# Convolution moved into the attention stage, half of the output weights loaded there, and the first tile taken first in the expert stage

## The chip, the cores and the metric

The kernel runs on one core of a Trainium2 chip. The metric is the device time of one execution in microseconds (us). TensorE is PE in the profile (its weight loads PEld), VectorE is DVE, ScalarE is ACT, GpSimd is POOL and SyncE is SP.

## The reference, cut to what matters

A trunk of two layers works on 640 tokens of width 1024: 128 context tokens (tile 0) and 512 latent tokens (tiles 1 to 4). Each layer computes, in float32:

```
h   = rms_norm(x) * (1 + scale1) + shift1
z   = h @ w_in                                  # 1024 x 2720
o_a = rwkv7(z); o_b = latent attention(z); o_c = grouped attention(z)
u   = c_gate * x_in                             # short convolution over the tokens
o_d = b_gate * (u[t-1] * w0 + u[t] * w1 + u[t+1] * w2 + conv_b)
x   = x + gate1 * (concat(o_a, o_b, o_c, o_d) @ w_out)
h2  = rms_norm(x) * (1 + scale2) + shift2
q   = h2 @ peer_wq                              # 8 heads, two halves each
    # scores against 2 x 128 keys, the best 16 of each half, the best 16 pairs: 128 experts a token
x   = x + gate2 * sum_k gelu(U[idx_k] . h2) * share_k * V[idx_k]
```

U and V are tables of 16384 rows of 4 KB for each layer. Every token needs 128 rows of each.

## The kernel before, in words

Per layer the program runs stages one after another, each closed by a barrier of all engines (`stage`, L139): the recurrent stage, `stage_mix`, `stage_attention`, `stage_experts`. Within a stage each engine has a list of instructions written out by hand, and semaphores order the engines.

**`stage_mix` (L988).** Six steps: five token tiles and the cached context. GpSimd computes the powers of -1/2 (L1182, L1186, L1202) that normalise rows and, between them, the convolution of the tile before (`convolve`, L1164 to 1178): per tile seven operations on 128x256, three multiplications by a tap (L1174) and four that add or multiply (L1178). All read and write SBUF. They need the shifted copies of u that SP makes by DMA at the start of the stage. VectorE does the row work of each step (L1277 to 1341).

**`stage_attention` (L1368).** 40 units, a tile and a head each: scores on TensorE (L1411, L1413), the maximum (L1477) and its negative (L1479) on VectorE, the exponential on ScalarE (L1457), transposes (L1438) and the product with the values (L1423) on TensorE, the copy (L1499), the reciprocal (L1502) and the scaling (L1487) on VectorE. GpSimd has nothing to do. SP loads the gates (L1398). The eight units of the context tile have one block of 128 keys, the other 32 have five.

**`stage_experts` (L1615).** At its start:

- SP loads both halves of w_out (L1684, 2 MB each), the first block of peer_wq, the keys, the second block of peer_wq (L1685 to 1687).
- TensorE transposes o chunk by chunk, eight chunks, each for all five tiles (L1988 for tile 0, L1990 for tiles 1 to 4). ScalarE copies tile 0's part to hT (L1827), VectorE the rest (L2071).
- TensorE then makes output products 0, 1 and 2 (`output(i)`, L1935 to 1942; product i is tile i//2, half i%2; 8 matmuls of 128x512 each). VectorE multiplies each by its gate (`gate_output`, L2066) and GpSimd adds it to x (`add_output`, L1725).
- With products 0 and 1 tile 0 is done: square sum (L1783), rstd (L1729, L1732), scaling (L2075), transposes (L1956), shift and scale (L2078). VectorE's scaling stands behind the gate of product 2 in its list.
- `first(n)` makes tile 0's queries and scores for two heads (L1971, L1980). VectorE ranks them in 20 steps (`rank_step`, L1530) and gives 32 expert numbers a token.
- GpSimd then issues a gather for each expert slot (L1770): 128 rows of 4 KB, one for each token. 128 gathers of U and then 128 of V for each of the five tiles, into a ring of 13 buffers. A gather waits until the row set that it replaces is used.
- VectorE forms the dot products with U (L2087). Rows of V are summed half by TensorE (L2051), half by VectorE (L2112). Before V can be used, ScalarE takes the exponentials of tile 0's best scores (L1847). They stand in its list behind the last copy of the other tiles' scores.
- The other tiles' output products, their normalisation and their queries (L1917) and scores (L1928) are made by TensorE under tile 0's gathers. `ADD_BEFORE`, `RSTD_BEFORE` and `GATE_BEHIND` say before which gather, or behind which dot product, an add, an rstd or a gate stands.

```
ADD_BEFORE = {2: 3, 7: 4, 12: 5, 18: 6, 22: 7, 26: 8, 30: 9}
RSTD_BEFORE = {4: 1, 14: 2, 24: 3, 31: 4}
GATE_BEHIND = {1: 4, 6: 5, 12: 6, 16: 7, 18: 8, 20: 9}
```

SBUF is full, so areas are used again: `m.w[0]` and `m.w[1]` are the two halves of one area of 32 KB a partition. In the attention stage it holds queries, keys and values up to column 7168. `m.rows` holds the constants of a layer, the taps and the bias of the convolution among them. In the expert stage its first 4096 columns hold the keys, two buffers, and scores.

Of the kernel before, what the change touches and what calls it, by code (L numbers as in the profile page):

```python
# [19 lines left out]
P = 128  # L20
# [967 lines left out]
def stage_mix(nc, m, l):  # L988
# [3 lines left out]
    with stage(nc) as sem:  # L992
# [22 lines left out]
        with nc.Block() as block:  # L1015
# [145 lines left out]
            def _(eng):  # L1161
                conv = Order(eng, conv_ordered)

                def convolve(t, first, end):  # L1164

                    if t < 0:
                        return
                    before, after, u = m.conv_before[:, t, :], m.conv_after[:, t, :], m.conv_u[:, t, :]
                    if t == 0 and first == 0:
                        eng.wait_ge(shifted, 96)  # L1170
                    for k in range(first, end):
                        if k < 3:
                            ap = (after, before, u)[k]
                            conv.mark(eng.tensor_tensor(ap, ap, row(m, "conv_w", (2, 0, 1)[k] * GW, GW), ALU.mult))  # L1174
                        else:
                            other = (before, u, row(m, "conv_b"), m.z[:, t, ZB:ZB + GW])[k - 3]
                            conv.after(0)
                            conv.mark(eng.tensor_tensor(after, after, other, ALU.mult if k == 6 else ALU.add))  # L1178

# [19 lines left out]
                for i in range(STEPS):  # L1199
# [10 lines left out]
                conv.after(0)  # L1210
# [157 lines left out]
def stage_attention(nc, m, l):  # L1368
# [17 lines left out]
    with stage(nc) as sem:  # L1386
# [4 lines left out]
        gates_loaded = sem("gates_loaded")  # L1391
        inverse, done = Marks(sem("sum_inverse"), "unit"), Marks(sem("attention_done"), "unit")
        with nc.Block() as block:
            @block.sync
            def _(eng):
                for g in range(2):
                    for s in range(2):
                        eng.dma_start(m.gate[:, g, s, :], m.gates[l, g, s].partition_broadcast(P)).then_inc(gates_loaded, 16)  # L1398
                eng.wait_ge(gates_loaded, 64)

# [214 lines left out]
def stage_experts(nc, m, l):  # L1615
# [10 lines left out]
    ADD_BEFORE = {2: 3, 7: 4, 12: 5, 18: 6, 22: 7, 26: 8, 30: 9}  # L1626
    RSTD_BEFORE = {4: 1, 14: 2, 24: 3, 31: 4}
    with stage(nc) as sem:
        sems = RankSemaphores(sem)
        w_out_loaded = [sem(f"w_out_loaded{b}") for b in range(2)]  # L1630
        o_turned = Marks(sem("o_turned"), "chunk")
        o_kept_v, o_kept_a = Marks(sem("o_kept_vector"), "chunk"), Marks(sem("o_kept_scalar"), "chunk")
# [45 lines left out]
        with nc.Block() as block:  # L1678
            @block.sync
            def _(eng):  # L1680
                w_out = at_layer(m.inp["w_out"], l).rearrange("(c p) n -> p c n", p=P)
                src = at_layer(m.inp["peer_wq"], l).rearrange("(c p) n -> p c n", p=P)
                for n in range(2):
# [216 lines left out]
            def _(eng):  # L1900
# [34 lines left out]
                def output(i):  # L1935
                    t, n = i // 2, i % 2
                    if t == 0:
                        eng.wait_ge(w_out_loaded[n], 16)
# [429 lines left out]
```

## Time and profile before

| | us |
|---|---|
| median of 3 runs | 4997.46 (4996.35 to 4998.36) |
| the profiled execution | 4998.08 |
| its span | 4996.3 |

| engine | busy us | share of the span |
|---|---|---|
| TensorE | 3135.7 | 63% |
| VectorE | 3904.6 | 78% |
| ScalarE | 770.0 | 15% |
| GpSimd | 2769.8 | 55% |

The span is the time from the first to the last instruction of the profiled execution; 1.8 us lie around it. The shares are means over stages with different limits, so what a change in one stage is worth is read from that stage. The mean granted clock of TensorE is 0.843 of full speed. Layer 0's mix stage runs from 622.3 us, its attention stage from 713.6 us, its expert stage from 822.7 us.

### The profile page before, as it was taken

To read this page: it belongs to the slowest core of one execution; us is meant where nothing else is said; L and a number is where in the kernel's file an instruction comes from. 1 tells how busy PE (TensorE), PEld (TensorE's weight loads), DVE (VectorE), ACT (ScalarE), POOL (GpSimd) and SP (SyncE) were. 2 spreads that over 40 slices of the span, in tenths; PEclk is the share of its full clock that TensorE was granted. 3 is DMA by queue.
4 is the path that set the end of the run, shared out by engine and by line. 5 is a ranking of instruction groups with operands and counts; after the bars stand their busy time and mean duration, and the time that the engine had idled before them with its cause. 6 is when DMAs were issued, how large, how long until landed. Compare 5 with 4: busy or idle time off the path is not lost. (4 is left out here: it accounts for less than half of the span.)

```text
span 4996.3 us, 39271 instructions
## 1 busy us (share of the span) xinstructions
PE 3135.7 (63%) x11894; PEld 1704.7 (34%) x11894; DVE 3904.6 (78%) x7390; ACT 770.0 (15%) x1904; POOL 2769.8 (55%) x2867
## 2 busy tenths in 40 slices
PE   8989869897045063277977995989713605407237
PEld 3368836542011021023425883754201202102012
DVE  6947674998997997978754666579889799799875
ACT  2112252211010010012111224321100101001001
POOL 0013240667777777766661224056777777767776
PEclk9989969999578597598998996999966958759669
DMA  8600012899999999999993001269999999999999
GB/s 308 226 17 2 3 33 76 315 411 409 410 399 409 409 399 407 398 410 390 417 381 115 2 1 36 76 248 410 409 409 400 409 409 395 410 409 399 410 399 365
DMA packets 434889, 1491.66 MB, mean 299 GB/s; under 512 B 47212, under 2 KB 55524, under 8 KB 433910
## 3 DMA queue, kind: packets, MB, share of 16 engines
q0 software_dynamic: 368640, 1342.34, 67.7%
q1 hardware_dynamic: 66040, 146.81, 8.2%
q8 instruction: 97, 1.59, 0.1%
q14 instruction: 112, 0.92, 0.1%
HBM read 1480.92 MB, written 5.44 MB: 297 GB/s over the span
## 5 line engine op out<-in xcount | busy, mean ns | idle before, releaser
L2051 PE MATMUL ps<-z,o 128*128 128x512 f32 x2356 | 1156.4, 618 | 516.9 <-DMA z<-in_peer_v,experts 333.6
L2087 DVE CUSTOM_DVE_ANT_0 z<-z,ps 128x1024 f32<-128x1024 f32 x1176 | 1414.4, 1218 | 77.2 <-DMA z<-in_peer_u,experts 38.5
L1770 POOL DMA_INDIRECT z<-in_peer_u,experts x1176 | 1113.5, 947 | 495.4 <-issue 214.5
L1770 POOL DMA_INDIRECT z<-in_peer_v,experts x1178 | 1115.1, 947 | 443.3 <-issue 274.1
L2112 DVE SCALAR_TENSOR_TENSOR ps<-z,state,ps 128x1024 f32<-128x1024 f32 x579 | 743.0, 1283 | 330.7 <-DMA z<-in_peer_v,experts 330.4
L2051 PEld LDWEIGHTS ps<-z,o 128*128 128x128 f32 x2356 | 411.3, 192 | 1256.4 <-ACT o L1890 712.9
L1905 PE MATMUL ps<-const,hT 128*128 128x128 f32 x80 | 17.8, 396 | 1035.4 <-ACT o L1890 1035.4
L1890 ACT ACTIVATE o<-const,state 128x128 f32<-128x128 f32 x640 | 244.5, 399 | 1070.0 <-PE ps L2051 1065.4
L1905 PEld LDWEIGHTS ps<-const,hT 128*128 128x128 f32 x80 | 14.4, 207 | 1040.7 <-ACT o L1890 1019.1
L1917 PE MATMUL ps<-hT,w 128*128 128x512 f32 x512 | 223.7, 592 | 0.0
L844 POOL TENSOR_TENSOR kn<-kn,neg_half 128x4 f32<-128x4 f32 x20 | 20.1, 1007 | 341.7 <-DVE kn L887 313.1
L854 POOL TENSOR_TENSOR w<-w,const 128x512 f32<-128x512 f32 x60 | 86.6, 1449 | 220.2 <-DVE w L876 122.7
L463 DVE SCALAR_TENSOR_TENSOR o<-gate,cond,o 128x1024 f32<-128x1024 f32 x160 | 192.4, 1275 | 10.2 <-DMA gate<-in_w_mod 10.2
L854 POOL TENSOR_TENSOR hT<-hT,const 128x512 f32<-128x512 f32 x60 | 85.6, 1432 | 205.4 <-DVE hT L876 103.6
L400 PE MATMUL ps<-w,hT 128*128 128x512 f32 (+1 forms) x480 | 189.4, 552 | 4.1 <-ACT hT L322 4.1
L1884 ACT ACTIVATE state<-state 128x128 f32<-128x128 f32 x10 | 3.1, 308 | 1172.3 <-DVE state L2093 1172.3
L1725 POOL TENSOR_TENSOR x<-x,rows 128x512 f32<-128x512 f32 x20 | 26.4, 1321 | 275.8 <-DVE rows L2066 275.5
L2033 PE MATMUL ps<-w,hT 128*128 128x512 f32 (+1 forms) x384 | 148.9, 551 | 3.0 <-ACT hT L1870 3.0
L1942 PE MATMUL ps<-w,hT 128*128 128x512 f32 x320 | 143.2, 608 | 5.0 <-DMA w<-in_w_out 5.0
L1917 PEld LDWEIGHTS ps<-hT,w 128*128 128x128 f32 x512 | 95.4, 190 | 111.0 <-issue 111.0
L400 PEld LDWEIGHTS ps<-w,hT 128*128 128x128 f32 x480 | 86.5, 192 | 102.5 <-issue 98.0
L1477 DVE TENSOR_REDUCE small<-ps 128x1 f32<-128x640 f32 (+1 forms) x80 | 57.4, 718 | 70.2 <-PE ps L1413 57.0
(434 smaller groups left out, 5234.5 us busy)
## 6 DMA issues: line engine op xcount, KB each, us to landing
gate<-in_w_mod SPq DMA_DIRECT2D x80, 512.0 KB, 4.5
w<-in_w_in SPq DMA_DIRECT2D x15, 2048.0 KB, 11.4
z<-in_peer_v,experts POOLq DMA_INDIRECT x1178, 12.0
z<-in_peer_u,experts POOLq DMA_INDIRECT x1176, 13.6
w<-in_peer_wq SPq DMA_DIRECT2D x8, 2048.0 KB, 19.4
w<-in_w_out SPq DMA_DIRECT2D x4, 2048.0 KB, 10.7
z<-in_peer_wq SPq DMA_DIRECT2D x4, 2048.0 KB, 16.9
rows<-in_rows SPq DMA_DIRECT2D x2, 2272.5 KB, 14.6
```

What stands on the lines that cost most here:

```text
L400: mm = eng.matmul(m.ps[:, 4 + i % 4, 0:cols], m.hT[:, c, t * P:(t + 1) * P], m.w[n % 2][:, c, 0:cols], start=(c == 0), stop=(c == KC - 1))
L463: eng.scalar_tensor_tensor(total, m.mod_piece[i % BUFFERS], m.cond[:, c, s:s + 1], m.mod_bias if c == 0 else total, ALU.mult, ALU.add).the ...
L854: eng.tensor_tensor(heads4(m.ct[d][j % 2][:, :]), m.lh[d][:, :].rearrange("p (h k x) -> p h k x", h=4, k=2)[:, :, 0, :], bc(const(m, f"lev ...
L1477: eng.tensor_reduce(m.small[:, u % 2:u % 2 + 1], scores, AX.X, ALU.max).then_inc(most.sem, most.one("raw", u))
L1770: eng.indirect_dma_start(slot, None, at_layer_rows(table), bass.IndirectOffsetOnAxis(ap=m.experts[:, t % 2, k:k + 1], axis=0)).then_inc(lo ...
L1890: eng.activation(m.diag[:, (done + q) % DIAGS, :], const(m, "ident"), ACT.Copy, scale=m.weight[:, 2 * q:2 * q + 1]).then_inc(diags_ready, 1)
L1917: mm = eng.matmul(m.ps[:, 6 + j % 2, :], m.w[p % 2][:, c, j % PER * P:(j % PER + 1) * P], m.hT[:, c, P:TOK], start=(c == 0), stop=(c == KC ...
L1942: mm = eng.matmul(m.ps[:, 4 + i % 2, :], m.hT[:, c, t * P:(t + 1) * P], m.w[n][:, c, :], start=(c == 0), stop=(c == KC - 1))
L2033: mm = eng.matmul(m.ps[:, 6 + i % 2, 0:cols], m.hT[:, c, t * P:(t + 1) * P], m.w[n % 2][:, c, 0:cols], start=(c == 0), stop=(c == KC - 1))
L2051: mm = eng.matmul(m.ps[:, 4 + n, :], m.diag[:, (done + q) % DIAGS, :], row_j[:, n * 512:(n + 1) * 512], start=(q == 0), stop=(q == SLOTS / ...
L2087: eng.tensor_tensor_reduce(row_j, row_j, h_rows, 1.0, 0.0, ALU.mult, ALU.add, m.acts[:, k:k + 1]).then_inc(used_v, 1)
L2112: ins = eng.scalar_tensor_tensor(acc, row_j, m.weight[:, k:k + 1], acc, ALU.mult, ALU.add)
```

## The change

1. `convolve` leaves `stage_mix`. The same 35 operations a layer become GpSimd's list in `stage_attention`.
2. SP, in `stage_attention`, waits for these 35 operations and then loads the first half of w_out into the first 4096 columns of `m.rows`, which nothing reads from then on. `stage_experts` loads the second half only. The areas are renamed to match: `m.we[0]` is in `m.rows`, `m.we[1]` is `m.w[1]`, and what lay in `m.rows` in the expert stage (keys, buffers, scores, four late ring buffers) now lies in the area of `m.w[0]`.
3. In `stage_experts` tile 0's eight transposes come first, kept by one 128x512 copy on ScalarE and one on VectorE. Output products 0 and 1 follow, then the transposes of the other tiles for chunks 0 to 4, the transposes of tile 0's normalised rows, chunks 5 and 6, `first(0)` with chunk 7 behind its queries, `first(1)`, and products 2 to 9.
4. Product 2 moves behind the first gathers' start. The lists that place the adds, the rstds and the gates have an entry more.

```diff
 stage_mix, gpsimd
-                    convolve(i - 1, 0, 2)
                     if i + 2 < TILES:
                         first_norm(i + 2)
-                    convolve(i - 1, 2, 4)
                     if i + 1 < TILES:
                         out_norm(i + 1)
-                    convolve(i - 1, 4, 7)
-                conv.after(0)
 stage_attention
+                eng.wait_ge(conv_ordered, 7 * TILES)
+                eng.dma_start(m.we[0], w_out[:, :, 0:512]).then_inc(w_out_loaded, 16)
...
+            @block.gpsimd
+            def _(eng):
+                conv = Order(eng, conv_ordered)
+                for t in range(TILES):
...
+                    for tap, k in ((after, 2), (before, 0), (u, 1)):
+                        conv.mark(eng.tensor_tensor(tap, tap, row(m, "conv_w", k * GW, GW), ALU.mult))
+                    for other, op in ((before, ALU.add), (u, ALU.add), (row(m, "conv_b"), ALU.add), (m.z[:, t, ZB:ZB + GW], ALU.mult)):
+                        conv.after(0)
+                        conv.mark(eng.tensor_tensor(after, after, other, op))
 stage_experts
-    ADD_BEFORE = {2: 3, 7: 4, 12: 5, 18: 6, 22: 7, 26: 8, 30: 9}
-    RSTD_BEFORE = {4: 1, 14: 2, 24: 3, 31: 4}
+    ADD_BEFORE = {2: 2, 7: 3, 12: 4, 17: 5, 22: 6, 26: 7, 28: 8, 30: 9}
+    RSTD_BEFORE = {9: 1, 19: 2, 27: 3, 31: 4}
...
-                for n in range(2):
-                    eng.dma_start(m.w[n], w_out[:, :, n * 512:(n + 1) * 512]).then_inc(w_out_loaded[n], 16)
+                eng.dma_start(m.we[1], w_out[:, :, 512:1024]).then_inc(w_out_loaded, 16)
...
                 add_output(0)
                 add_output(1)
                 rstd(0)
-                add_output(2)
...
 scalar
-                for c in range(KC):
-                    eng.wait_ge(*o_turned("chunk", c))
-                    eng.activation(m.hT[:, c, 0:P], m.ps[:, 2 * (c % 2) + 1, 0:P], ACT.Copy).then_inc(o_kept_a.sem, o_kept_a.one("chunk", c))
+                eng.wait_ge(*o_first_turned("half", 0))
+                eng.activation(m.hT[:, 0:4, 0:P], m.ps[:, 2, :].rearrange("p (c n) -> p c n", c=4), ACT.Copy).then_inc(o_first_kept_a, 1)
...
 tensor
+                for b in range(2):
+                    for c in range(4):
+                        mm = eng.transpose(m.ps[:, 2 + b, c * P:(c + 1) * P], m.o[:, 0, (4 * b + c) * P:(4 * b + c + 1) * P], ident)
+                    mm.then_inc(o_first_turned.sem, o_first_turned.one("half", b))
+                eng.wait_ge(o_first_kept_a, 1)
+                eng.wait_ge(o_first_kept_v, 1)
+                output(0)
+                output(1)
+                for c in range(5):
+                    turn_rest(c)
                 turn_x(0)
+                turn_rest(5)
+                turn_rest(6)
                 first(0)
                 first(1)
+                eng.wait_ge(*o_kept("chunk", KC - 1))
                 turn_h(0)
-                for i in range(3, 6):
+                for i in range(2, 6):
                     output(i)
...
 vector
-                for i in range(3):
+                eng.wait_ge(*o_first_turned("half", 1))
+                eng.tensor_copy(m.hT[:, 4:8, 0:P], m.ps[:, 3, :].rearrange("p (c n) -> p c n", c=4)).then_inc(o_first_kept_v, 1)
+                for i in range(2):
                     gate_output(i)
+                for c in range(5):
+                    keep_rest_o(c)
...
                 ins.then_inc(h_first, 1)
+                for c in range(5, KC):
+                    keep_rest_o(c)
...
-                GATE_BEHIND = {1: 4, 6: 5, 12: 6, 16: 7, 18: 8, 20: 9}
+                GATE_BEHIND = {1: 3, 6: 4, 11: 5, 17: 6, 20: 7, 22: 8, 24: 9}
...
-                gate_output(3)
+                gate_output(2)
```

## Rows read from the trace of the kernel before

**Rows 1.** The page: DMA's busy tenths in 40 slices of 125 us; the gathers' queue.

```profile
DMA  8600012899999999999993001269999999999999
...
q0 software_dynamic: 368640, 1342.34, 67.7%
```

**Rows 2.** Busy by engine in stretches: length, PE, PEld, DVE, ACT, POOL; clock, DMA share, GB/s.

```profile
652.81:668.09 15.28, 9.51 (x25) 4.84 (x24) 13.59 (x29) 9.36 (x31) 11.07 (x11) 0.50 0.00 0
...
724.40:822.70 98.30, 96.94 (x614) 76.88 (x614) 63.48 (x167) 37.84 (x100) 0.00 (x0) 0.96 0.00 1
...
940.00:960.00 20.00, 15.87 (x126) 15.71 (x127) 19.78 (x47) 4.33 (x11) 7.42 (x9) 0.83 0.83 303
...
1000.00:1020.00 20.00, 20.00 (x59) 9.77 (x58) 20.00 (x64) 2.99 (x5) 13.25 (x15) 1.00 1.03 412
```

**Rows 3.** One line's instructions: duration in ns min/median/max, first and last start, form.

```profile
L1178 POOL TENSOR_TENSOR o<-o,z x30: 722/787/1320, 660.5 to 3105.0; 128x256 f32<-128x256 f32 x30
...
L1336 DVE TENSOR_TENSOR state<-state,rows x10: 426/830/832, 642.3 to 3091.5; 128x256 f32<-128x256 f32 x10
...
L985 DVE TENSOR_TENSOR gate<-gate,hT x8: 358/562/773, 636.4 to 3074.2; 128x192 f32<-128x192 f32 x8
...
L945 DVE TENSOR_TENSOR w<-ps,w x50: 681/690/692, 311.0 to 2974.2; 128x512 f32<-128x512 f32 x50
...
L2071 DVE COPY hT<-ps x16: 678/686/692, 823.5 to 3221.8; 128x512 f32<-128x512 f32 x16
```

**Rows 4.** Timeline, end of layer 0's mix: start, us, engine, line, operation, idle before.

```profile
687.49 1.09 DVE L1307 TENSOR_TENSOR hT<-hT,rows 128x768 f32<-128x768 f32 x1 [0.31 <-ACT hT L1085]
...
695.46 0.65 DVE L1299 TENSOR_SCALAR small<-small 128x8 f32<-128x8 f32 x1
...
710.81 0.59 ACT L1127 ACTIVATE w<-ps 96x512 f32<-96x512 f32 x1 [1.94 <-PE ps L1252]
...
711.84 0.72 POOL L1178 TENSOR_TENSOR o<-o,z 128x256 f32<-128x256 f32 x1
```

**Rows 5.** Timeline, start of layer 0's expert stage.

```profile
822.72 1.01 SPq L1684 DMA_DIRECT2D w<-in_w_out  x2
...
831.80 23.69 PE L1942 MATMUL ps<-w,hT 128*128 128x512 f32 x48 [3.05 <-DMA w<-in_w_out]
...
848.66 0.69 DVE L2066 TENSOR_TENSOR rows<-ps,gate 128x512 f32<-128x512 f32 x1 [6.17 <-PE ps L1942]
...
852.27 0.58 POOL L1732 TENSOR_TENSOR small<-small,neg_half 128x1 f32<-128x1 f32 x1
...
856.13 0.74 DVE L2075 TENSOR_SCALAR o<-x,small 128x1024 f32<-128x1024 f32 x1
...
860.75 9.04 PE L1971 MATMUL ps<-hT,z 128*128 128x128 f32 x64 [2.73 <-DVE hT L2078]
...
888.23 1.21 POOL L1770 DMA_INDIRECT z<-in_peer_u,experts  x1 [30.22 <-DVE experts L1590]
```

**Rows 6.** The same of layer 1: the chain's first piece, then the timeline.

```profile
3215.71 7.83 DMA w<-in_w_out
...
3239.27 0.69 DVE L2066 TENSOR_TENSOR rows<-ps,gate 128x512 f32<-128x512 f32 x1 [6.17 <-PE ps L1942]
...
3251.37 10.36 PE L1971 MATMUL ps<-hT,z 128*128 128x128 f32 x64 [2.73 <-DVE hT L2078]
...
3280.14 1.09 POOL L1770 DMA_INDIRECT z<-in_peer_u,experts  x1 [31.52 <-DVE experts L1590]
```

**Rows 7.** Timeline, tile 0 under its gathers in layer 0: GpSimd, TensorE, ScalarE.

```profile
939.24 1.08 POOL L1770 DMA_INDIRECT z<-in_peer_u,experts  x1 [0.19 <-issue]
...
943.44 8.97 PE L1971 MATMUL ps<-hT,w 128*128 128x128 f32 x64 [11.24 <-DMA w<-in_peer_wq]
...
950.76 0.94 POOL L1770 DMA_INDIRECT z<-in_peer_u,experts  x1 [10.45 <-DVE experts L1590]
...
1095.08 0.31 ACT L1847 ACTIVATE o<-o 128x128 f32<-128x128 f32 x1 [5.91 <-DVE o L1537]
```

More of the change, by code:

```diff
@@ L1162, in _ @@
                 conv = Order(eng, conv_ordered)
[L1164 to L1176, printed above, removed]
-                            conv.after(0)
-                            conv.mark(eng.tensor_tensor(after, after, other, ALU.mult if k == 6 else ALU.add))
                 def first_norm(t):
@@ L1398, in _ @@
                         eng.dma_start(m.gate[:, g, s, :], m.gates[l, g, s].partition_broadcast(P)).then_inc(gates_loaded, 16)
+                w_out = at_layer(m.inp["w_out"], l).rearrange("(c p) n -> p c n", p=P)
+                eng.wait_ge(conv_ordered, 7 * TILES)
+                eng.dma_start(m.we[0], w_out[:, :, 0:512]).then_inc(w_out_loaded, 16)
                 eng.wait_ge(gates_loaded, 64)
+                eng.wait_ge(w_out_loaded, 16)
+            @block.gpsimd
+            def _(eng):
+                conv = Order(eng, conv_ordered)
+                for t in range(TILES):
+                    before, after, u = m.conv_before[:, t, :], m.conv_after[:, t, :], m.conv_u[:, t, :]
+                    for tap, k in ((after, 2), (before, 0), (u, 1)):
[3 more added lines that the diff above has]
+                        conv.mark(eng.tensor_tensor(after, after, other, op))
+                conv.after(0)
             @block.tensor
@@ L1936, in output @@
                     t, n = i // 2, i % 2
-                    if t == 0:
-                        eng.wait_ge(w_out_loaded[n], 16)
+                    if t == 0 and n == 1:
+                        eng.wait_ge(w_out_loaded, 16)
                     if i >= 2:
@@ L1967, in first @@
                         wait_wq(WQ_ORDER.index(n))
-                    w = m.wq_first[n] if n < 2 else m.w[WQ_ORDER.index(n)]
+                    w = m.wq_first[n] if n < 2 else m.we[WQ_ORDER.index(n)]
                     for i in range(PER):
@@ L1973, in first @@
                     mm.then_inc(first_q.sem, first_q.one("block", n))
+                    if n == 0:
+                        turn_rest(KC - 1)
                     eng.wait_ge(*first_q_kept("block", n))
@@ L2258, in place @@
     oall = m.o[:, :, :].rearrange("p t n -> p (t n)")
-    m.xs = [oall[:, 4096:5120], m.rows[:, 2048:3072]]
+    m.we = [m.rows[:, 0:4096].rearrange("p (c n) -> p c n", c=KC), m.w[1]]
+    m.xs = [oall[:, 4096:5120], wall[:, 2048:3072]]
     m.wq_first = [zall[:, at:at + 4096].rearrange("p (c n) -> p c n", c=KC) for at in (9 * D, 4 * D)]
-    m.out_tmp = [m.rows[:, 3072 + b * 512:3072 + (b + 1) * 512] for b in range(2)]
-    m.keys = m.rows[:, 0:2048].rearrange("p (j n) -> p j n", j=2 * HEADS)
-    m.score_out = m.rows[:, 2048:4096].rearrange("p (t j n) -> p t j n", t=TILES - 1, j=4)
+    m.out_tmp = [wall[:, 3072 + b * 512:3072 + (b + 1) * 512] for b in range(2)]
+    m.keys = wall[:, 0:2048].rearrange("p (j n) -> p j n", j=2 * HEADS)
+    m.score_out = wall[:, 2048:4096].rearrange("p (t j n) -> p t j n", t=TILES - 1, j=4)
     m.score_kept = {n: at.rearrange("p (t j n) -> p t j n", t=TILES - 1, j=4) for n, at in (
-        (2, m.gate[:, 0, :, :].rearrange("p s n -> p (s n)")), (0, m.rows[:, 2048:4096]), (1, wall[:, 0:2048]))}
+        (2, m.gate[:, 0, :, :].rearrange("p s n -> p (s n)")), (0, wall[:, 2048:4096]), (1, m.rows[:, 0:2048]))}
     m.score_tile = m.const[:, P:P + 2048].rearrange("p (j n) -> p j n", n=NKEY)
@@ L2289, in place @@
     m.acts, m.cube, m.weight, m.share = m.state[0][:, 0, :], m.state[0][:, 1, :], m.state[1][:, 0, :], m.state[1][:, 1, :]
-    m.late_ring = ([m.rows[:, s * D:(s + 1) * D] for s in range(4)] + [m.gate[:, 0, s, :] for s in range(2)]
+    m.late_ring = ([wall[:, s * D:(s + 1) * D] for s in range(4)] + [m.gate[:, 0, s, :] for s in range(2)]
                    + [m.const[:, P + s * D:P + (s + 1) * D] for s in range(2)]
```

46 lines of the change are left out of this document (20 added, 26 removed).

## The prediction

> **What bounds the kernel now.** I read the page first. The DMA engines are nine tenths busy or more from the eighth slice to the twenty-first and again from the twenty-eighth on, and the gathers' queue alone takes 67.7% of the span [rows 1]. So most of the time is the gathers of two expert stages: 2560 gathers and 1342 MB. A window at 1000 us shows 412 GB/s and VectorE busy throughout [rows 2]. In such a stretch nothing that the change touches can be won. What can be won is time ahead of the first gather: if a layer's first gather comes earlier, the stream behind it comes earlier. Between the streams the stages follow each other behind barriers, so time saved in the mix or attention stage counts in full.
>
> In the **mix stage** VectorE is busy 13.59 of the 15.28 us of one step, and ScalarE 9.36 [rows 2]. VectorE bounds it, and it is slowed: the same 128x256 operation takes 426 ns alone and 830 ns while a convolution step runs on GpSimd, and another takes 358 and 773 [rows 3]. The stage ends with GpSimd's last step at 711.84 + 0.72 = 712.56. The last other work ends at 710.81 + 0.59 = 711.40 [rows 4].
>
> The **head of the expert stage** in layer 0 is one chain: SP issues the w_out loads at 822.72, the first lands after about 9.05 us, three products run from 831.80, the second is gated at 848.66, rstd is ready at 852.27 + 0.58 = 852.85, but VectorE scales at 856.13 only, behind the third product's gate; queries start at 860.75 and the first gather at 888.23 [rows 5]. Layer 1 has the same chain [rows 6].
>
> **The mix stage without the convolution.** In each of the first two steps that have it, five VectorE operations are lengthened by 0.40 us or a little more [rows 3], 2.0 us. The first two stand ahead of a wait for ScalarE that takes some of it back, while GpSimd's powers come sooner: I take 1.9 each, 3.8. In the third step the wait for ScalarE stands already (0.31) and hides what is ahead of it; behind it are the lengthened L1307 (1.09) and one more operation, and a small one of 0.65 us on eight columns [rows 4], nearly all of it a hold: 1.0 together. In the fourth, four operations behind the wait lose 0.4 to 0.5 each: 1.8. The tail gives 0.1 of a stretched operation and 712.56 - 711.40 = 1.16. Sum: 3.8 + 1.0 + 1.8 + 0.1 + 1.2 = 7.9 a layer, **15.8**. Bounds: the tail alone, 2.4 for both layers, and every stretched operation in full, about 20.
>
> **The attention stage with the convolution.** 35 operations at 787 ns [rows 3] are 27.5 us, inside 109 us in which GpSimd had nothing. The 2 MB load behind them needs the 7.8 to 9.05 us that such a load takes [rows 5, 6], and ends near 40 us of the stage; SP has only its end wait behind it. Nobody waits for either until the barrier. What could cost is VectorE held by GpSimd. The stretched operations above all read two SBUF tiles. The 128x512 one that reads PSUM and SBUF took 681 to 692 ns in all 50 instances, in a stage in which GpSimd works on 128x512 tiles too [rows 3]. Attention's VectorE operations read PSUM, or one column. I take 0. A gain is excluded, since nothing there waits for GpSimd; above stands the full hold, worked out as a rival.
>
> **The head of the expert stage.** Eight transposes replace forty ahead of the products. They take 1.1 us (eight of the 64 query matmuls that took 9.04 [rows 5]), and the copy of the second half 0.69 [rows 3]: with semaphores product 0 starts 2.0 us after the stage's start. It takes 6.87 us at full clock: the three ended at 831.80 + 23.69 = 855.49, the second at 848.60 by its gate, so the third took 6.89 and the first, at the same rate for the second, 9.9 [rows 5]. It ends at +8.87. The half of w_out that product 1 needs is now the first load: it lands at +9.05 in layer 0 and +7.83 in layer 1. Product 1 then ends at +15.95 and +15.74. Before it ended at 848.60 (+25.88) and 3239.22 (+23.51) [rows 5, 6]. Won: 9.9 and 7.8.
>
> Behind product 1, rstd is ready 852.85 - 848.60 = 4.25 us later. VectorE has five new copies of 0.69 there, from +0.75, each behind four transposes: done at +4.2 to +4.6. I take +4.5 for the scaling, where it was 856.13 - 848.60 = 7.5: **3.0** won a layer. From the scaling to the queries nothing changes (4.6 us). TensorE's chunks 5 and 6 (0.5 each) lie beside VectorE's eight shifts. Chunk 7's transposes and copies 5 to 7 lie beside the queries and their copy. The keys and the two blocks of peer_wq follow one load instead of two on SP's queue, so they come sooner. First queries before: 9.04 and 10.36 us [rows 5, 6]; I take them unchanged.
>
> So the first gather comes 12.9 us sooner in layer 0 and 10.8 in layer 1. Given back: one more gate (0.69) stands on VectorE between the first and the second ranking. GpSimd's adds 8 and 9 move before gathers 28 and 30; gate 9 behind dot product 24 is ahead of three dot products and a third of the second ranking's steps, so gathers 30 and 31 still go out ahead of gather 32, which waited 10.45 us for that ranking [rows 7]. Net **22.3** in both layers.
>
> **Sum:** 15.8 + 0 + 22.3 = 38.1. The profiled execution took 4998.08, which gives 4960.0; it stands 0.6 above the median of 4997.46.
>
> **Does the stream take it?** Tile 0's V rows need ScalarE's exponentials, which stand behind the other tiles' last scores. ScalarE idled 5.91 us before them [rows 7]. TensorE now makes eight instead of seven products after the first queries, 6.9 us, so that chain moves by 12.9 - 6.9 = 6.0 while VectorE's moves by 12.2: 0.3 us late, if nothing else helps. But TensorE idled 11.24 us for a peer_wq block there [rows 7], issued when product 8 is done. That load now runs further into the stretch at 940 us in which DMA moves only 303 GB/s [rows 2], and should be quicker. I take no loss.
>
> **Rivals.**
>
> (a) *VectorE is held in attention.* One SBUF operation on eight columns took 0.65 us beside GpSimd [rows 4]. If the negation and the reciprocal of a unit were held like that, about 0.24 us each in the eight short units of a layer, where no slack hides them: 8 x 2 x 0.24 = 3.8 a layer, 4968. Against it: those have a single column. By the Trainium skill (GPSIMD Engine Reference, Specifications) the two engines contend when a VectorE instruction runs in a 2-port mode or has two SBUF inputs. If the one-column operations were in such a mode, this case would hold; no row here shows them beside GpSimd.
>
> (b) *TensorE's clock.* Product 0 took 3.1 us more than the warm 6.87 after a wait of 3.05, layer 1's first queries 10.36 where layer 0's took 9.04 [rows 5, 6]: starts at 1.2 GHz. The new order has sparse work ahead of both. If product 0 stays cold in both layers and layer 0's queries lose 1.3 more: 3.1 x 2 + 1.3 = 7.5, 4967.5. Against it: only 0.9 of the 3.05 us of waiting is left ahead of product 0. By the Trainium skill (TensorE: Matmul & The Clock Gate, "What's actually happening") the throttled clock is the default and recent activity releases it; by that rule it is this case whenever attention's tail and eight transposes do not suffice.
>
> (c) *The other tiles are late.* If the peer_wq load is not quicker and the margin of 5.91 is less than it looks, V rows start up to 6 us late a layer: 4972.
>
> (d) *The stream doesn't take the earlier start*, being bound by something issued later; only the mix stage's 15.8 is left: 4982.
>
> (e) *Slower.* Every convolution step holds attention's VectorE, and by it each unit, for its whole 787 ns: 70 x 0.787 = 55 us against 38.1, 5015. The decision point is 38.1 / 70 = 0.54 us a step. For it: the two-tile operations were held for 0.40. Against it: the PSUM reader never was, and in the 32 long units, 98.30 us, VectorE is busy 63.48 [rows 2], so part of a hold would be hidden.
>
> **How the numbers follow.** Forecast 0.68, (a) 0.10, (b) 0.10, (c) 0.06, (d) 0.03, (e) 0.03. The forecast's own spread is 4952 (mix at its upper bound, queries warm) to 4966. With (a), (b) and (c) the range goes up to 4975; (d) and (e) are left out. A measurement tells 0.2% (10 us) from no change. Faster by more: all but (e) and a hold near the decision point, 0.95; within 0.02; slower 0.03.
>
> **What would show it.** Right: no convolution in the mix stage and a step of some 13.4 us where it was 15.28; attention as long as before with 35 GpSimd operations in it; product 0 at +2, product 1 ending near +16, the scaling 4.5 behind it; first gather at 65.5 - 12.9 = 52.6 us after the stage's start (layer 1: 64.4 - 10.8 = 53.6); later stages unchanged in length. Wrong: attention longer by more than 2 us; a wait ahead of product 1 beyond 0.5 us; a wait of VectorE for ScalarE's exponentials with DMA below 400 GB/s behind it.

## The result and the profile after

The changed kernel takes **4959.03 us** (median of 4 runs, 4956.22 to 4961.09) against 4996.91 (4 runs, 4993.97 to 4998.36) of the kernel before on the same chip: ratio 0.9925, 95% interval 0.9913 to 0.9938, 38 us less. The prediction said 4960, with a spread of its own from 4952 to 4966 and up to 4975 with three of its rivals. The profiled execution took 4958.27, its span 4956.5 against 4996.3: 39.8 less, where the sum said 38.1. Five more runs, in a later comparison, gave 4959.94 (ratio 0.9924, 0.9910 to 0.9937). In the experiments one execution of one kernel was slow (5786.87 us at a granted clock of 0.686) and counts in no ratio.

All of it lies ahead of the streams of gathers. A stage starts with SP's first load, and "rest" runs from a layer's first gather to the next layer's mix stage, or to the end:

| us | mix | attention | expert stage to first gather | rest |
|---|---|---|---|---|
| before, layer 0 | 91.31 | 109.11 | 65.51 | 2127.3 |
| after, layer 0 | 82.85 | 108.42 | 54.23 | 2128.0 |
| before, layer 1 | 91.33 | 108.86 | 64.43 | 1716.2 |
| after, layer 1 | 82.84 | 109.41 | 52.13 | 1715.8 |

(Mix 16.9 + attention 0.1 + heads 23.6 - rest 0.3 - a start of layer 0's mix 0.5 later = 39.8.)

**The mix stage.** First GpSimd's powers of layer 0, one a step, then the lengthened 128x256 operation of [rows 3] by its form:

```profile
653.35 1.74 POOL L1186 TENSOR_TENSOR small<-small,neg_half 128x8 f32<-128x8 f32 x1 [3.37 <-DVE small L1279]
666.61 1.74 POOL L1186 TENSOR_TENSOR small<-small,neg_half 128x8 f32<-128x8 f32 x1 [3.37 <-DVE small L1279]
679.88 1.74 POOL L1186 TENSOR_TENSOR small<-small,neg_half 128x8 f32<-128x8 f32 x1 [3.37 <-DVE small L1279]
691.56 1.74 POOL L1186 TENSOR_TENSOR small<-small,neg_half 128x8 f32<-128x8 f32 x1 [1.82 <-DVE small L1279]
699.64 1.01 POOL L1186 TENSOR_TENSOR small<-small,neg_half 128x4 f32<-128x4 f32 x1 [6.34 <-DVE small L1279]
```

```profile
L1316 DVE TENSOR_TENSOR state<-state,rows x10: 424/424/426, 642.9 to 3067.2; 128x256 f32<-128x256 f32 x10
```

The distance of two powers is one step: 13.26 and 13.27 us where it was 15.28 twice, then 11.68 and 8.08 where it was 12.81 and 9.91. The operation that took 830 ns in its median takes 424 in all ten.

**Attention.** VectorE's negation and reciprocal, the first half's load and GpSimd's convolution, each by its line:

```profile
L1476 DVE TENSOR_SCALAR small<-small x80: 152/153/155, 706.9 to 3183.4; 128x1 f32<-128x1 f32 x80
...
L1499 DVE RECIPROCAL small<-small x80: 150/152/155, 708.3 to 3185.9; 128x1 f32<-128x1 f32 x80
...
L1382 SPq DMA_DIRECT2D rows<-in_w_out x2: 389/390/390, 732.1 to 3105.6; - x2
...
DMA to landing us min/median/max: 7.5/7.6/7.6
...
L1392 POOL TENSOR_TENSOR z<-z,rows x20: 716/721/724, 706.4 to 3101.6; 128x256 f32<-128x256 f32 x20
```

In the kernel before, with nothing beside them, the first two took 153 and 152 ns in the median and 155 at most: the same. The load is issued at 732.08, 26.4 us after the stage's start, and has landed 74 us before its end.

The stage is 0.69 us shorter in layer 0 and 0.55 longer in layer 1. Its first 20 us, in the kernel before and in the changed one, show what differs (columns as in [rows 2], the clock third from the right):

```profile
713.61:733.61 20.00, 18.97 (x69) 14.01 (x69) 11.72 (x49) 7.50 (x30) 0.00 (x0) 0.55 0.27 106
3106.85:3126.85 20.00, 18.97 (x71) 14.26 (x72) 11.95 (x49) 7.71 (x31) 0.00 (x0) 0.56 0.30 106
...
705.69:725.69 20.00, 18.97 (x73) 14.19 (x74) 12.34 (x51) 8.25 (x32) 18.80 (x27) 0.59 0.29 107
3079.18:3099.18 20.00, 18.96 (x66) 13.86 (x67) 11.44 (x47) 7.37 (x30) 18.79 (x27) 0.53 0.29 107
```

TensorE's clock is at the lower level at the end of the mix stage, and it rises 18.1 and 17.6 us into the attention stage of the kernel before, 16.5 and 18.7 us into that of the changed one. The longer the low stretch, the longer the stage: 109.11, 108.86, 108.42 and 109.41.

**The head of the expert stage**, TensorE's timeline of layer 0, where the stage starts at 814.11:

```profile
814.15 1.73 PE L1989 MATMUL ps<-const,o 128*128 128x128 f32 x8 [1.17 <-PEq L151]
816.75 9.32 PE L1936 MATMUL ps<-rows,hT 128*128 128x512 f32 x16 [0.88 <-DVE hT L2078]
825.91 7.03 PE L1936 MATMUL ps<-w,hT 128*128 128x512 f32 x16
...
838.01 1.75 PE L1950 MATMUL ps<-const,w 128*128 128x128 f32 x8 [1.60 <-DVE w L2084]
839.56 1.91 PE L1984 MATMUL ps<-const,o 128*128 128x128 f32 x8
842.50 7.41 PE L1965 MATMUL ps<-hT,z 128*128 128x128 f32 x64 [1.02 <-DVE hT L2087]
```

The same of layer 1, from 3188.59:

```profile
3188.64 1.06 PE L1989 MATMUL ps<-const,o 128*128 128x128 f32 x8 [1.17 <-PEq L151]
3190.58 8.54 PE L1936 MATMUL ps<-rows,hT 128*128 128x512 f32 x16 [0.88 <-DVE hT L2078]
3198.96 7.03 PE L1936 MATMUL ps<-w,hT 128*128 128x512 f32 x16
...
3211.07 1.09 PE L1950 MATMUL ps<-const,w 128*128 128x128 f32 x8 [1.60 <-DVE w L2084]
```

Product 0 starts 2.64 and 1.99 us into the stage; in layer 0 it was 9.08. Nothing waits for the second half of w_out, which lands 8.8 us after its issue at the stage's start, while product 1 starts at +11.8 and +10.4. But product 0 takes 9.32 and 8.54 us where product 1 takes 7.03, and in layer 0 the transposes around it take 1.73 and 1.75 for eight where layer 1's take 1.06 and 1.09. The granted clock in short stretches (columns as in [rows 2]) shows why: in layer 0 it is at the lower level, 1.2 GHz, from the first transposes to about 821. In layer 1 it falls in the pause of 0.88 us ahead of product 0.

```profile
814.40:815.40 1.00, 1.00 (x7) 1.00 (x6) 0.00 (x0) 0.34 (x1) 0.00 (x0) 0.50 0.25 14
...
820.00:821.00 1.00, 1.00 (x2) 0.34 (x1) 0.00 (x0) 0.00 (x0) 0.00 (x0) 0.50 1.08 412
821.00:822.00 1.00, 1.00 (x3) 0.42 (x2) 0.00 (x0) 0.00 (x0) 0.00 (x0) 0.89 1.03 389
822.00:823.00 1.00, 1.00 (x4) 0.47 (x3) 0.00 (x0) 0.00 (x0) 0.00 (x0) 1.00 1.05 410
...
3189.70:3190.58 0.88, 0.00 (x1) 0.03 (x1) 0.69 (x1) 0.20 (x1) 0.00 (x0) 0.71 0.65 135
```

VectorE gates product 1 and scales, layer 0:

```profile
832.98 0.69 DVE L2070 TENSOR_TENSOR w<-ps,gate 128x512 f32<-128x512 f32 x1 [6.18 <-PE ps L1936]
...
837.21 0.75 DVE L2084 TENSOR_SCALAR w<-x,small 128x1024 f32<-128x1024 f32 x1
```

**Under the gathers** of tile 0, the rows that answer to [rows 7], on GpSimd, TensorE and ScalarE:

```profile
868.34 1.21 POOL L1765 DMA_INDIRECT z<-in_peer_u,experts  x1 [31.17 <-DVE experts L1587]
...
922.35 1.26 POOL L1721 TENSOR_TENSOR x<-x,w 128x512 f32<-128x512 f32 x1 [2.54 <-DVE w L2070]
...
931.47 0.94 POOL L1765 DMA_INDIRECT z<-in_peer_u,experts  x1 [3.62 <-DVE experts L1587]
```

```profile
926.94 9.05 PE L1965 MATMUL ps<-hT,rows 128*128 128x128 f32 x64 [7.76 <-DMA rows<-in_peer_wq]
```

```profile
1077.30 0.31 ACT L1841 ACTIVATE o<-o 128x128 f32<-128x128 f32 x1 [4.55 <-DVE o L1534]
```

Gather 32 waits 3.62 us instead of 10.45, but it is the same ranking that it waits for, 19.3 us sooner than before: its predecessors now go out later behind the adds (2.54 us for a gate), and use up part of the time. ScalarE still idles 4.55 us before the exponentials, so V rows wait for VectorE's ranking as before.

### The profile page after: what moved, and what is told of

Its sections match the earlier page's. It is cut to its first block and busy times, and to the rows that moved or that the text cites. A ratio compares the mean times of both kernels' runs of the same rounds, so it can differ in the third digit from the quotient of the medians.

```text
span 4956.5 us, 39249 instructions
## 1 busy us (share of the span) xinstructions
PE 3134.1 (63%) x11894; PEld 1703.1 (34%) x11894; DVE 3888.6 (78%) x7392; ACT 767.4 (15%) x1890; POOL 2759.1 (56%) x2867
## 5 line engine op out<-in xcount | busy, mean ns | idle before, releaser
L1899 PE MATMUL ps<-const,hT 128*128 128x128 f32 x80 | 17.8, 396 | 1033.2 <-ACT o L1884 1033.2
L463 DVE SCALAR_TENSOR_TENSOR o<-gate,cond,o 128x1024 f32<-128x1024 f32 x160 | 192.4, 1278 | 12.1 <-DMA gate<-in_w_mod 12.1
L400 PE MATMUL ps<-w,hT 128*128 128x512 f32 (+1 forms) x480 | 189.6, 553 | 4.1 <-ACT hT L322 4.1
L1721 POOL TENSOR_TENSOR x<-x,w 128x512 f32<-128x512 f32 x20 | 25.4, 1272 | 212.0 <-DVE w L2070 211.8
L1911 PE MATMUL ps<-hT,rows 128*128 128x512 f32 x256 | 111.9, 593 | 0.0
L1911 PE MATMUL ps<-hT,w 128*128 128x512 f32 x256 | 111.9, 593 | 0.0
L2098 DVE DVE_READ_ACCUMULATOR2_ANT state<- 128x1 f32 x1280 | 104.9, 82 | 0.0
L948 DVE TENSOR_TENSOR w<-ps,w 128x512 f32<-128x512 f32 x120 | 82.6, 689 | 17.8 <-PE ps L721 17.5
## 6 DMA issues: line engine op xcount, KB each, us to landing
rows<-in_peer_wq SPq DMA_DIRECT2D x4, 2048.0 KB, 16.9
```

Source lines behind the costliest of these rows:

```text
L400: mm = eng.matmul(m.ps[:, 4 + i % 4, 0:cols], m.hT[:, c, t * P:(t + 1) * P], m.w[n % 2][:, c, 0:cols], start=(c == 0), stop=(c == KC - 1))
L463: eng.scalar_tensor_tensor(total, m.mod_piece[i % BUFFERS], m.cond[:, c, s:s + 1], m.mod_bias if c == 0 else total, ALU.mult, ALU.add).the ...
L948: eng.tensor_tensor(m.invT[d][:, :], bank(d, 3), m.invT[d][:, :], ALU.add).then_inc(vec[d].sem, vec[d].one(f"xy{j}", n))
L1911: mm = eng.matmul(m.ps[:, 6 + j % 2, :], m.we[p % 2][:, c, j % PER * P:(j % PER + 1) * P], m.hT[:, c, P:TOK], start=(c == 0), stop=(c == K ...
L2098: eng.tensor_tensor_reduce(row_j, row_j, h_rows, 1.0, 0.0, ALU.mult, ALU.add, m.acts[:, k:k + 1]).then_inc(used_v, 1)
```

## The experiments

Ten runs were made on three chips, two of them repeats of a kernel that had run. On the first (the changed kernel again, and the three with more transposes) the kernel before takes 4997.55. On the two others it takes 5481. What differs is the streams alone: from layer 0's first gather to layer 1's mix stage 2393 to 2414 us instead of 2128, at 332 GB/s from 1100 to 1500 us in one of them, where the changed kernel has 406 on the first chip. The mix stages agree to 0.14 us on all three. So ratios are taken within a chip, and the parts are read from the stages. The kernel before left a trace on the first chip only. That the chip doesn't set the stages is borne out by the changed kernel, whose heads are 54.23 and 52.13 there and 54.39 and 52.29 on another chip with steps added on GpSimd:

| us | mix, layer 0, 1 | attention | to first gather | ratio to before |
|---|---|---|---|---|
| convolution alone moved | 82.84, 82.87 | 108.41, 109.38 | 61.59, 65.00 | 0.9961 (0.9949 to 0.9974) |
| the same again | 82.82, 82.84 | 108.42, 109.77 | 61.57, 63.54 | 0.9953 (0.9937 to 0.9969) |
| early load, old order | 82.93, 82.95 | 109.71, 109.34 | 60.19, 61.61 | 0.9963 (0.9951 to 0.9975) |
| new order, no early load | 82.84, 82.84 | 109.76, 109.60 | 59.32, 58.89 | 0.9944 (0.9928 to 0.9960) |
| 105 steps on GpSimd | 82.96, 82.96 | 108.43, 109.71 | 54.39, 52.29 | 0.9929 (0.9913 to 0.9946) |
| changed kernel again | 82.83, 82.84 | 108.43, 109.78 | 54.20, 52.31 | 0.9924 (0.9910 to 0.9937) |
| chunks 0 and 1 first | 82.83, 82.83 | 109.81, 109.64 | 51.90, 52.42 | 0.9924 (0.9910 to 0.9937) |
| more transposes | 82.82, 82.86 | 109.32, 110.65 | 50.97, 50.68 | 0.9912 (0.9898 to 0.9925) |
| and shifts split | 82.83, 82.85 | 109.33, 110.75 | 49.69, 49.56 | 0.9908 (0.9893 to 0.9923) |
| without those in attention | 82.84, 82.83 | 108.42, 109.45 | 52.15, 49.71 | 0.9916 (0.9898 to 0.9934) |

### The convolution alone

The edit, from the kernel before:

```diff
 stage_mix, gpsimd
-                    convolve(i - 1, 0, 2)
...
 stage_attention
+            @block.gpsimd
+            def _(eng):
+                conv = Order(eng, conv_ordered)
...
```

> The kernel before with the convolution alone moved to the attention stage; no early load, the order of the expert stage as before. Theory (the parts act on separate stretches): each mix stage 8.5 us shorter, as in the changed kernel, attention as long as before to within 1 us, the first gathers 65.5 and 64.4 us after the start of their stages as before. 2 x 8.5 = 17 less than 4997: 4980. Rival (VectorE is held in attention beside GpSimd): attention about 3.8 us a layer longer, 4988. Rival (the gain in the mix stage came from somewhere else than the convolution): mix stages as before, 4997.

5458.36 us (6 runs) against 5481.16, ratio 0.9961; the stages up to the first gathers are 20.5 us shorter than before. The mix stages have all that the changed kernel's have, so the 8.5 us a layer are the convolution's leaving and nothing else. Attention is 0.7 us shorter in layer 0 and 0.5 longer in layer 1, as in the changed kernel. Unexpected was layer 0's head, 61.59 us where the kernel before has 65.51. So the same kernel ran again:

> The kernel with the convolution alone moved, a second time. In its first execution the profile gave mix stages of 82.8 us, attention of 108.4 and 109.4, but a head of 61.6 us in layer 0 where the kernel before has 65.5. Theory (the difference is where TensorE's low clock falls, in the forty transposes or in product 0): mix and attention as in the first execution, layer 0's head either 61.6 or 65.5, and the time 17 to 21 us below the kernel before. Rival (moving the convolution shortens the head too): 61.6 again.

61.57 again, 5456.54 against 5481.21. TensorE in the first execution, layer 0, where the stage starts at 814.31:

```profile
814.53 1.06 PE L1983 MATMUL ps<-const,o 128*128 128x128 f32 x4
...
819.35 0.60 PE L1983 MATMUL ps<-const,o 128*128 128x128 f32 x4
...
822.28 20.87 PE L1935 MATMUL ps<-w,hT 128*128 128x512 f32 x48 [0.78 <-DVE hT L2064]
```

Four transposes take 1.06 us at first, then 0.60: the low clock falls on the transposes. They end later, the load has landed meanwhile, and the three products take 20.87 us where they took 23.69 [rows 5]. The clock was low either way; here it was low over work that hides behind the load. In layer 0 it repeats to 0.02 us, so it isn't luck of one execution. So the rival has layer 0 right: the head is shorter with the convolution gone, by where the low clock falls. In the kernel before it fell 8.0 us into this stage, here 0.1 us into it. In layer 1 nothing of the kind is seen, 65.00 and 63.54 where the kernel before has 64.43, and the clock falls 8.3 and 8.7 us into the stage where it fell after 7.8.

### Load and order taken apart

First the changed kernel without the early load:

```diff
 stage_attention, sync
-                eng.wait_ge(conv_ordered, 7 * TILES)
-                eng.dma_start(m.we[0], w_out[:, :, 0:512]).then_inc(w_out_loaded, 16)
 stage_experts, sync
+                eng.dma_start(m.we[0], w_out[:, :, 0:512]).then_inc(w_out_first, 16)
                 eng.dma_start(m.we[1], w_out[:, :, 512:1024]).then_inc(w_out_loaded, 16)
```

> The changed kernel with the first half of w_out loaded at the start of the expert stage again, ahead of the second half; the new order stays. Theory (product 0 needs its load and nothing hides it): product 0 starts with the landing, 9.05 and 7.8 us after the stage's start, instead of 2.64 and 1.99, at the low clock after the wait (9.9 us), and the second half has landed by then. Product 1 ends near +26 and +24.7 instead of +18.8 and +17.4. First gathers 7.2 us later in both layers, at +61.4 and +59.4; 4959 + 14.4 = 4973. Rival (the head is set by VectorE and the transposes, the load is hidden): under 2 us a layer, 4959 to 4963.

Heads 5.1 and 6.8 us longer than the changed kernel's, 7.2 expected. TensorE, layer 0:

```profile
813.72 1.06 PE L1986 MATMUL ps<-const,o 128*128 128x128 f32 x8 [1.17 <-PEq L151]
821.40 9.27 PE L1933 MATMUL ps<-rows,hT 128*128 128x512 f32 x16 [6.61 <-DMA rows<-in_w_out]
```

Product 0 starts 7.73 us into the stage instead of 9.05, and after 6.61 us of waiting it takes 9.27, no more than the changed kernel's 9.32 after 0.88: the low clock cost the changed kernel as much as the long wait would have.

Then the changed kernel with the expert stage's old order:

```diff
-                output(0)
-                output(1)
-                for c in range(5):
-                    turn_rest(c)
-                turn_x(0)
-                turn_x(0)
-                turn_rest(5)
-                turn_rest(6)
+                for i in range(3):
+                    output(i)
+                turn_x(0)
```

(the forty transposes of the kernel before ahead of it, its lists of gates, adds and rstds behind it)

> The changed kernel with the expert stage in the order of before (forty transposes, then products 0 to 2, the scaling behind the gate of product 2); convolution and early load as changed. Theory: the transposes end near +7, product 0 then runs at full clock (6.9 us) because TensorE never paused long, product 1 ends near +21, the scaling 7.5 us behind it at +28.4, where the changed kernel has it at +23.1. First queries as before, 9.04 and 10.36 us instead of 7.41. One gate less between the rankings gives 0.7 back. Sum 6 to 8 us a layer, 4959 + 14 = 4973. The early load by itself would then be worth about 7 of the 21 us that the expert heads win, and the order the other 14. Rival (the load was the whole of it, the order brings nothing): 4959 to 4961.

Heads 6.0 and 9.5 us longer, 6 to 8 expected; the rival (the load is the whole) falls. TensorE, layer 0 from 813.91:

```profile
820.72 7.13 PE L1938 MATMUL ps<-rows,hT 128*128 128x512 f32 x16 [0.78 <-DVE hT L2067]
827.69 7.03 PE L1938 MATMUL ps<-w,hT 128*128 128x512 f32 x16
834.55 7.03 PE L1938 MATMUL ps<-rows,hT 128*128 128x512 f32 x16
843.03 1.09 PE L1952 MATMUL ps<-const,w 128*128 128x128 f32 x8 [1.44 <-DVE w L2071]
846.86 8.80 PE L1967 MATMUL ps<-hT,z 128*128 128x128 f32 x64 [2.73 <-DVE hT L2074]
```

Products at full clock, no wait for a load; but they start at +6.8, product 2 stands ahead of the scaling, and the queries take 8.80 (10.24 in layer 1) behind a pause of 2.73.

The two parts need each other. Against the convolution alone (mean of its two executions, 61.6 and 64.3) the early load wins 1.4 and 2.7 us, the order 2.3 and 5.4. Together they win 7.4 and 12.1, 3.7 and 4.0 more than the two sums of 3.7 and 8.1 (the clock's dips, a microsecond or two, are in all of these). The shares expected, 7 us for the load and 14 for the order, don't come out: neither has a share of its own. In the old order the forty transposes cover the load nearly; in the new one without the load, product 0 waits for it.

### Three times the steps on GpSimd

```diff
                         conv.mark(eng.tensor_tensor(after, after, other, op))
+                    for _ in range(14):
+                        conv.after(0)
+                        conv.mark(eng.tensor_tensor(before, before, u, ALU.add))
```

> The changed kernel with 70 more GpSimd operations of 128x256 a layer behind the 35 in the attention stage, adding dead data to dead data; the load of w_out behind them. GpSimd then works for about 79 of the 109 us, beside the long units too. Theory (VectorE is not held by them there): attention as long as in the changed kernel to within 1 us, the load still lands ahead of the stage's end, 4959. Rival (one-column operations of VectorE are held by 0.24 us each): up to 2 x 0.24 us in each of some 28 units, 13 us a layer, 4985. Rival (each operation holds a unit for its whole length): 70 x 0.787 = 55 us a layer, 5069.

Attention 108.43 and 109.71 us, the changed kernel's again 108.43 and 109.78, with 105 steps on GpSimd instead of 35. The load is issued at 788.10, the stage ends at 813.82. VectorE's reciprocal in this run, by its line:

```profile
L1502 DVE RECIPROCAL small<-small x80: 152/154/155, 708.0 to 3471.7; 128x1 f32<-128x1 f32 x80
```

Both rivals fall: a step costs attention nothing that shows, also beside the long units. Ratio 0.9929, as the changed kernel's on the first chip.

### TensorE's clock in the head

The changed kernel ran again beside three others, each with the edit of the one before it.

> The changed kernel once more, as the measure for the three runs beside it. Theory: mix stages 82.8 us, heads of the expert stage 54.2 and 52.1 us, about 40 us ahead of the kernel before on the same chip. Rival (the heads' lengths are luck of the clock in one execution): heads off by more than 2 us.

4959.94 us, heads 54.20 and 52.31 (54.23 and 52.13 in the first execution): product 0 took 9.36 and 8.73. The dips repeat, so the rival (luck of one execution) falls.

The first of the three:

```diff
+                for c in range(2):
+                    turn_rest(c)
                 eng.wait_ge(o_first_kept_a, 1)
                 eng.wait_ge(o_first_kept_v, 1)
                 output(0)
                 output(1)
-                for c in range(5):
+                for c in range(2, 5):
```

> The changed kernel with the transposes of the other tiles' chunks 0 and 1 ahead of product 0, in the wait of 0.88 us for tile 0's copies. Theory (TensorE's clock falls for want of work around the start of the stage): eight more transposes bring the clock back sooner, product 0 takes 8 us or less instead of 9.3 and 8.5, starts up to 0.8 us later, and the heads are 0 to 1 us shorter, 4957 to 4959 on the chip of the first comparison. Rival (the fall was decided in attention's last microseconds, and these transposes change nothing): product 0 as long as before and 0.2 to 0.8 us later, heads that much longer.

TensorE, layer 0 from 813.87:

```profile
813.91 1.06 PE L1991 MATMUL ps<-const,o 128*128 128x128 f32 x8 [1.17 <-PEq L151]
814.81 1.04 PE L1986 MATMUL ps<-const,o 128*128 128x128 f32 x8
815.85 7.11 PE L1938 MATMUL ps<-rows,hT 128*128 128x512 f32 x16
```

Eight transposes that have to be made anyway fill the pause, product 0 starts 1.98 us into the stage and takes 7.11 in both layers. The head of layer 0 is 2.3 us shorter, but its attention stage, whose work is the same, is 1.4 us longer: the clock rose 19.5 us into it, not 16.6. So layer 0 is not a clean comparison: the clock's rises and falls lay differently from the stage before on. In layer 1 attention is as long to 0.1 us, and the head is 0.1 longer: product 0 wins 1.6 there, and the queries lose it, 9.04 instead of 7.41. The time is 4960.08, no less than 4959.94; 1 us in the stages is below what five runs tell. Next, twelve transposes that nobody reads at each of two more pauses:

```diff
                 attended(N - 1)
+                for j in range(12):
+                    eng.transpose(m.ps[:, 0, j % 4 * P:(j % 4 + 1) * P], m.prob[0][:, 0:P], const(m, "ident"))
...
+                for j in range(12):
+                    eng.transpose(m.ps[:, 7, j % 4 * P:(j % 4 + 1) * P], m.o[:, 1, 0:P], ident)
                 turn_x(0)
```

> As the run before, and with transposes whose results nobody reads: twelve on TensorE behind attention's last product, and twelve ahead of the transposes of tile 0's normalised rows. Theory (the low clock in the head follows TensorE's pauses of 1 to 2 us): at full clock product 0 takes 6.9 to 7.2 us and the transposes of the normalised rows 1.1, heads at 51.5 and 50.5 us, 4 us less in sum. Rival (the clock does not follow these pauses): product 0 stays at 8.5 to 9.3, heads as in the run before or up to 0.5 us longer for the added transposes.

Product 0 7.11 and 7.10, queries 7.41 in both layers, heads 50.97 and 50.68: 3.2 and 1.6 us less than the changed kernel's where 4 in sum were expected. Here the clock rises 16.5 us into layer 0's attention, as in the changed kernel (16.6), so this comparison is clean. Those behind attention cost 0.9 us a layer there, which no theory had counted. 4953.67 (4951.72 to 4955.15) against 4959.94 (4958.03 to 4961.62): the runs of the two don't overlap. Of these 6.3 us the stages up to the first gathers account for 3.1 (4.9 in the heads, less 1.8 in attention); the rest lies in the streams and is not explained.

```diff
+                eng.wait_ge(*tile_turned("tile", 0))
+                for c in range(4, KC):
+                    ins = eng.activation(m.hT[:, c, 0:P], m.ps[:, 2 + c // 4, c % 4 * P:(c % 4 + 1) * P], ACT.Identity,
+                                         scale=m.mod_col[l][:, 3, 0, c:c + 1], bias=m.mod_col[l][:, 2, 0, c:c + 1])
+                ins.then_inc(h_first, 1)
                 keep_first(0)
...
-                for c in range(KC):
+                for c in range(4):
...
```

> As the run before, and half of the eight shift and scale operations ahead of tile 0's queries on ScalarE instead of VectorE. Theory (these eight, 2.65 us in a row, are all that TensorE waits for there): 1.2 us a layer less than the run before, 2.4 in sum; the queries stay at full clock. Rival (ScalarE's form of the operation with a scale and a bias a partition is as slow as two of VectorE's): no change.

TensorE, layer 0, the transposes of the normalised rows, chunks 5 and 6, and the queries:

```profile
835.59 1.09 PE L1957 MATMUL ps<-const,w 128*128 128x128 f32 x8 [0.29 <-DVE w L2095]
836.52 1.04 PE L1991 MATMUL ps<-const,o 128*128 128x128 f32 x8
838.28 7.41 PE L1972 MATMUL ps<-hT,z 128*128 128x128 f32 x64 [0.72 <-ACT hT L1827]
```

Heads 1.3 and 1.1 us shorter than the run before, 1.2 expected: the shifts were what TensorE waited for. 4952.73 us (4949.84 to 4953.02), the lowest median here, 7 us below the changed one on the same chip; from the run before it is 0.9 us, and the two ranges overlap. Last, the same without the twelve behind attention:

```diff
                 attended(N - 1)
-                for j in range(12):
-                    eng.transpose(m.ps[:, 0, j % 4 * P:(j % 4 + 1) * P], m.prob[0][:, 0:P], const(m, "ident"))
```

> The kernel with the split shift operations, without the twelve transposes behind attention's last product, which made both attention stages 0.9 us longer. Theory (the eight transposes of the other tiles ahead of product 0 are enough for the clock there, as they were by themselves): attention 0.9 us shorter in both layers, heads 49.7 and 49.6 us as with them, time 1 to 2 us less, 4951. Rival (the filler kept the clock up): product 0 takes 8.5 us or more in a layer, 4953 to 4956.

It ran on another chip, so it is judged by its stages. Attention is 0.9 and 1.3 us shorter, as expected. The head of layer 0 is 2.5 us longer, that of layer 1 as long. TensorE in layer 0, from 814.15:

```profile
814.19 1.75 PE L1994 MATMUL ps<-const,o 128*128 128x128 f32 x8 [1.17 <-PEq L151]
815.73 1.91 PE L1989 MATMUL ps<-const,o 128*128 128x128 f32 x8
817.44 7.23 PE L1941 MATMUL ps<-rows,hT 128*128 128x512 f32 x16
```

Product 0 has its full clock but for 0.1 us, and the sixteen transposes ahead of it don't: 3.7 us where 2.1 do. Neither theory had that. The clock rose 16.5 us into this attention stage, as in the changed kernel; there the low stretch at the head's start lasted 6.8 us, here 3.4. So at the same start the eight transposes of real work shorten the dip, and they don't prevent it. The sum over both layers is 0.4 us worse than with the twelve: they are worth about what they cost, and whether they are in or out is open.

## Why the prediction was right, point by point

**Mix: right, by its steps.** 2.0, 2.0, 1.1, 1.8 and, from the last power to the end, 1.5 us, where it had 1.9, 1.9, 1.0, 1.8 and 1.26; 8.5 a layer against 7.9. That a lengthened VectorE operation ahead of a standing wait brings next to nothing (the third step) fits these numbers.

**Attention: right.** -0.69 us in layer 0 and +0.55 in layer 1, where 0 was taken. This isn't GpSimd's. In the 20 attention stages here without added transposes the length goes with the time into the stage at which TensorE's clock rises: 108.4 at 16.2 to 16.6 us (105 steps on GpSimd among them), 108.9 and 109.1 at 17.6 and 18.1 (no step on GpSimd), 109.3 to 109.5 at 18.6 to 18.7, 109.6 to 109.8 at 19.1 to 19.5. The prediction has no term for it, and over two layers it comes to 0.1 us. The load ended 34 us into the stage; the terms given for it (27.5 and 7.8 to 9.05) make 35 to 37, not 40. Rival (a) falls with the 155 ns. By the Trainium skill (GPSIMD Engine Reference, Specifications) the engines contend when the VectorE instruction runs in a 2-port mode or has two SBUF inputs; the traces agree for two inputs (424 and 830 ns) and put the one-column operations outside of it (153 and 154). Rival (e) falls with the run of 105 steps. "A gain is excluded, since nothing there waits for GpSimd" stands for the engines; the load's leaving the head is counted there.

**Head: the sum was right (22.3 said; 11.3 + 12.3 = 23.6 to the first gathers, 0.7 given back in layer 0's stream and -0.4 in layer 1's, 0.69 a layer said), but three of its terms were wrong and offset each other, in the layers too: 12.9 and 10.8 said, 11.3 and 12.3 measured.** That they offset is luck.
- "It takes 6.87 us at full clock" failed: product 0 took 9.32 and 8.54, 2.4 and 1.7 more. The step took the duration of the third product in a row of three, and the shortness of the pause as cover. That was rival (b), given 0.10, in its part on product 0; its part on the queries went the other way. The pause wasn't what counted: in layer 0 the clock was low from the first transposes on, ahead of the pause of 0.88 us.
- "The second half lands at +9.05" holds TensorE up nowhere, since product 0 ends near +12 and +10.5. Products 1 end at +18.8 and +17.4 instead of +15.95 and +15.74; won 7.1 and 6.1 instead of 9.9 and 7.8.
- "First queries ... I take them unchanged" failed in the other direction: 7.41 us in both layers, 1.6 and 2.95 less than 9.04 and 10.36. The step had chunks 5 and 6 "beside VectorE's eight shifts" at no cost; they are also work in a pause that had been 2.73 us and is now 1.02 and 1.85. That this keeps the clock up is argued, not shown: with chunks 0 and 1 first, chunks 5 and 6 stand in the same place behind the same 1.86 us, and layer 1's queries took 9.04. What is shown is that no low stretch falls on these queries.
- The scaling stands 4.3 us behind product 1 (837.21 - 832.92), 4.5 said: right. In layer 0 0.7 of it is lost again, because the transposes of the normalised rows run at the low clock (1.75).

**Stream: right.** Rest 2128.0 and 1715.8 us against 2127.3 and 1716.2. Rival (c)'s wait didn't come: the peer_wq load was waited for 7.76 instead of 11.24 us, and the exponentials ran 17.8 us sooner. Rival (d) falls with them.

So the time was right by a mechanism that held and, by luck, two errors of clock with opposite signs: product 0's two losses and the transposes' make 4.8 us, the queries' two gains 4.6. With the queries as long as before, the time would have been near 4964, still in the range.

## What to carry to other kernels

A GpSimd operation that slows VectorE's operations on two SBUF tiles can cost nothing beside operations of another form: here 35 steps cost the mix stage 8.5 us and attention nothing, and one view of durations by line was enough to price that beforehand. A load issued early pays only if the order of the work can use it, and the order only if the load is there, so price them together. Where TensorE is the chain, its pauses of 1 to 3 us are a place for work that has to be done anyway; ask which work its low clock falls on, not only whether it falls, and read the stage before too: with eight transposes moved into the first pause the low clock fell on later work, and the time stayed at 4960.

## What was not expected of the hardware

- After attention, with TensorE at full clock up to its last microsecond, the clock was at the lower level within 2 us of sparse work, and for 3 to 4.5 us from the next product's start. With a pause of 0.88 us and with one of 6.61 us product 0 took the same (9.32, 9.27). In layer 0 the head repeats to 0.03 us (61.59 and 61.57; 54.23 and 54.20), in layer 1 to 1.5. Which work the low clock falls on differs between kernels (1.06 to 1.94 us for the same eight transposes). It goes with the stage before: where the clock rose 16.2 to 16.6 us into attention and no transposes were added behind it, it was low again by 0.4 us into the next stage (six of six); where it rose at 17.6 us or later, not before 1.4 us (14 of 14). What sets the time of the rise is open.
- On three chips the kernel before took 4997.55, 5481.16 and 5481.21 us. The 484 us are nearly all in the streams of gathers (332 to 369 GB/s in three stretches of 400 us on one of them, 399 to 406 on the first), while the mix stages agree to 0.14 us. Why is open.
